# Tile sizes of the prompt loop in a hybrid mLSTM and attention layer: 256 rows at both ends, 512 in the middle

## The reference

```python
h  = rmsnorm(x) * (1 + scale1) + shift1
z  = h @ w_in        # mLSTM q, k, v, o-gate, i-gate, f-gate; attention q, k, v
h_m  = mlstm_chunkwise(...)          # 4 heads x 128, recurrent matrix memory
attn = banded attention, 8 heads x 64, own chunk and 2 chunks before
x  = x + gate1 * (concat(h_m, attn) @ w_out)
x  = x + gate2 * (square(relu((rmsnorm(x) * (1 + scale2) + shift2) @ w_up)) @ w_down)
```

## Time and profile before

| | us |
|---|---|
| median of two runs | 2631.73 |
| the two runs | 2524.87 and 2738.6 |
| the profiled execution | 2528.94 |
| its span on the slowest core (core 5) | 2527.4 |
| spans of the eight cores | 2487.8 to 2527.4 |
| TensorE busy | 1952.1 (77%) |
| VectorE busy | 1124.4 (44%) |
| ScalarE busy | 873.3 (35%) |
| bytes moved by DMA | 267.74 MB, mean 106 GB/s |

### The profile page before, as it was taken

How to read it: one execution, slowest core, us unless ns; L and a number is a source line. 1 busy time by engine, 2 the same in 40 slices (tenths; PEclk the granted TensorE clock), 3 DMA queues, 4 the chain that set the end, 5 groups by cost and what they waited for, 6 DMA issues and landing times.

```text
span 2527.4 us, 33429 instructions; the slowest of 8 cores (2487.8 to 2527.4 us)
## 1 busy us (share of the span) xinstructions
PE 1952.1 (77%) x11094; PEld 917.5 (36%) x11094; DVE 1124.4 (44%) x2546; ACT 873.3 (35%) x2072; POOL 97.4 (4%) x137
## 2 busy tenths in 40 slices
PE   0353577856569798888888888988888889879796
PEld 0121233323324343444433433434444434334343
DVE  2116455544544545444444445454444444454420
ACT  0013465533344324332443334244324333342220
POOL 0000000000000000000000000010000000000101
PEclk9956788878789998999999989999999999999899
DMA  9764995201162235124422522262154225323545
GB/s 239 153 113 68 149 157 109 92 1 51 51 202 84 68 96 171 51 67 139 112 67 84 167 67 67 87 186 62 53 140 126 67 83 154 81 67 93 141 151 122
DMA packets 191866, 267.74 MB, mean 106 GB/s; under 512 B 7148, under 2 KB 168076, under 8 KB 190160
## 3 DMA queue, kind: packets, MB, share of 16 engines
q1 hardware_dynamic: 163840, 201.11, 25.6%
q0 software_dynamic: 27856, 64.50, 15.3%
HBM read 260.96 MB, written 51.38 MB: 124 GB/s over the span
## 4 chain that ended last, share of the span: by engine, by line
PE 56%; DVE 12%; ACT 12%; DMA 11%; issue 8%; DVEq 0%; ACTq 0%; SPq 0%; POOL 0%; POOLq 0%
PE psb L968 13%; PE psb L988 12%; PE psb L701 11%; PE psb L935 5%; PE psb L1007 4%; DVE sb_Eo L855 3%; PE psb L646 3%; DMA ym<-sb_ytmp 3%; DMA sb_uT<-w_in 2%; ACT sb_junk L608 2%; ACT sb_junk L843 1%; DMA sb_x<-xp 1%; ACT sb_qT L612 1%; ACT sb_mixT L923 1%; ACT sb_uT L1120 1%
## 5 line engine op out<-in xcount | busy, mean ns | idle before, releaser
L968 PE MATMUL psb<-sb_h2T,sb_fs 128*128 128x512 bf16 x2048 | 522.0, 396 | 22.3 <-DVE sb_ytmp L994 14.0
L988 PE MATMUL psb<-sb_fs,sb_uT 128*128 128x512 bf16 (+1 forms) x2112 | 505.3, 388 | 15.0 <-DMA sb_fs<-wdn_s 15.0
L701 PE MATMUL psb<-sb_win,sb_hT 128*128 128x512 bf16 (+2 forms) x1576 | 344.1, 366 | 6.4 <-DVE sb_Kp L710 4.2
L988 PEld LDWEIGHTS psb<-sb_fs,sb_uT 128*128 128x128 bf16 (+1 forms) x2112 | 199.5, 99 | 243.6 <-issue 35.9
L968 PEld LDWEIGHTS psb<-sb_h2T,sb_fs 128*128 128x128 bf16 x2048 | 195.4, 101 | 246.2 <-issue 57.9
L972 ACT ACTIVATE sb_uT<-psb 128x512 bf16<-128x512 f32 (+1 forms) x288 | 158.3, 550 | 329.5 <-PE psb L968 326.3
L973 DVE TENSOR_TENSOR sb_uT<-sb_uT 128x512 bf16<-128x512 bf16 (+1 forms) x288 | 112.8, 396 | 280.4 <-ACT sb_uT L972 246.0
L701 PEld LDWEIGHTS psb<-sb_win,sb_hT 128*128 128x128 bf16 (+1 forms) x1576 | 152.2, 99 | 159.5 <-issue 16.0
L935 PE MATMUL psb<-sb_wout,sb_mixT 128*128 128x512 bf16 (+1 forms) x528 | 127.8, 395 | 27.0 <-ACT sb_mixT L923 25.8
L886 ACT ACTIVATE sb_Pm<-psb 128x256 bf16<-128x256 f32 (+1 forms) x264 | 99.7, 378 | 94.7 <-PE psb L881 85.6
L735 DVE SCALAR_TENSOR_TENSOR sb_Chat<-sb_Chat,sb_rho_bc,psb 128x129 f32<-128x129 f32 x260 | 90.2, 347 | 78.9 <-PE psb L730 63.5
(11 more groups left out here) (190 smaller groups left out, 2134.0 us busy)
## 6 DMA issues: line engine op xcount, KB each, us to landing
sb_fs<-wup_s SPq DMA_DIRECT2D x72, 1024.0 KB, 5.3
sb_fs<-wdn_s SPq DMA_DIRECT2D x72, 1024.0 KB, 5.7
sb_x<-xp SPq DMA_DIRECT2D x32, 512.0 KB, 14.8
sb_x<-xm SPq DMA_DIRECT2D x32, 512.0 KB, 5.3
ym<-sb_x POOLq DMA_DIRECT2D x32, 512.0 KB, 5.7
ym<-sb_ytmp POOLq DMA_DIRECT2D x64, 256.0 KB, 4.5
sb_fs<-w_ada POOLq DMA_DIRECT2D x12, 1024.0 KB, 15.5
sb_uT<-w_in SPq DMA_DIRECT2D x8, 1412.0 KB, 11.4
```

Source lines behind the costliest of these rows:

```text
L701: i = e.matmul(pb[0:T, 0:ncols], lhsT=hsrc[:, kc, col_tok0:col_tok0 + T], rhs=win[:, kc, c0:c0 + ncols], start=(kc == 0), stop=(kc == KC - 1))
L968: i = e.matmul(pb[:, 0:NT], lhsT=sl[:, kc, j * 128:(j + 1) * 128], rhs=h2src[:, kc, 0:NT], start=(kc == 0), stop=(kc == KC - 1))
L988: i = e.matmul(pbs[bi][0:T, :], lhsT=uT[:, g * 8 + j, c0:c0 + T], rhs=sl[:, j, :], start=(g == 0 and j == 0), stop=(g == 3 and j == 7))
```

## The change

The list of tile sizes replaces the fixed 512 rows: two tiles of 256 rows (two blocks), six of 512 (four blocks), two of 256, ten tiles in all for the same 4096 rows. norm_T4, thread_B and thread_A take their number of blocks from the tile; gates and qk_feature_major get 256 or 512 columns; ffn_up gets 256 or 512 columns per matmul with the same number of matmuls and the same 16 weight loads per tile; ffn_down has half the matmuls in a small tile, with the same loads. The prefix loop and the sample are as before.

```diff
--- before.py
+++ after.py
@@ -603,16 +603,16 @@
                  r=[dstT.b, modT.b], w=[dstT.b], cost=0.7)
 
         def norm_T4(xts, dstT, n, r):
-            T = 128
-            for b in range(4):
+            nb = len(xts)
+            for b in range(nb):
                 S.op("act", lambda e, b=b: e.activation(out=junk2[:, :], in_=xts[b][:, :], func=AF.Square, accum_out=st4[:, b:b + 1]),
                      r=[xts[b].b], w=[st4.b], cost=1.1)
-            rstd_from_ss(st4[:, 0:4], st4[:, 4:8], D, st4)
-            for b in range(4):
+            rstd_from_ss(st4[:, 0:nb], st4[:, 4:4 + nb], D, st4)
+            for b in range(nb):
                 S.op("act", lambda e, b=b: e.activation(out=xn4[b], in_=xts[b][:, :], func=AF.Identity, scale=st4[:, 4 + b:5 + b]),
                      r=[xts[b].b, st4.b], w=[xn4b[b], (qT.b if b < 2 else kT.b)], cost=1.1)
             base = 0 if n == 0 else 24
-            for pair in range(2):
+            for pair in range(nb // 2):
                 pbs_ = {}
                 for b in (2 * pair, 2 * pair + 1):
                     pbs_[b] = nps()
@@ -1151,19 +1151,32 @@
             S.op("pool", lambda e: e.nop(), r=dram_out_bufs, force=True)
             S.emit()
             return nc
-        n_mt = NM // 512
         curh = [0]
 
+        if NM >= 1536:
+            sizes = [2, 2] + [4] * ((NM - 1024) // 512) + [2, 2]
+        else:
+            sizes = [2] * (NM // 256)
+        tiles = []
+        r0 = 0
+        for nb_ in sizes:
+            tiles.append((r0, nb_))
+            r0 += nb_ * 128
+        assert r0 == NM
+        n_mt = len(tiles)
+
         def thread_B(t):
+            row0, nb = tiles[t]
+            NT = nb * 128
             S.begin()
             xt = xt_next[0]
-            gtail = gates(512, T, 4, defer_tail=True)
-            qk_feature_major(512)
+            gtail = gates(NT, T, nb, defer_tail=True)
+            qk_feature_major(NT)
             gtail()
-            for b in range(4):
-                last = (t == n_mt - 1 and b == 3)
+            for b in range(nb):
+                last = (t == n_mt - 1 and b == nb - 1)
                 cur = curh[0]
-                mixer_block(T, b, b * 128, cur, 128, 0, last, cbf_ready=(b > 0), cbf_next=(b < 3))
+                mixer_block(T, b, b * 128, cur, 128, 0, last, cbf_ready=(b > 0), cbf_next=(b < nb - 1))
                 if last:
                     store("pool", knf, knf[:, :], okp_d)
                     store("pool", vf, vf[:, :], ovp_d)
@@ -1174,26 +1187,27 @@
             S.barrier("up%d" % (t - 1))
             blocks = []
             norm_T4(xt, h2T, 1, 0)
-            for b in range(4):
-                yd = ym_d[t * 512 + b * 128:t * 512 + (b + 1) * 128, :]
+            for b in range(nb):
+                yd = ym_d[row0 + b * 128:row0 + (b + 1) * 128, :]
                 yb = Buf("y"); dram_out_bufs.append(yb)
                 S.op("pool", lambda e, yd=yd, xb=xt[b]: e.dma_start(out=yd, in_=xb[:, :]), r=[xt[b].b], w=[yb], dma="y_" + xt[b].b.name)
                 blocks.append((yd, T, b * 128, yb))
             if t + 1 < n_mt:
-                xt_next[0] = [next_x(xm_d, (t + 1) * 512 + b * 128) for b in range(4)]
+                nrow0, nnb = tiles[t + 1]
+                xt_next[0] = [next_x(xm_d, nrow0 + b * 128) for b in range(nnb)]
                 norm_T4(xt_next[0], hT, 0, 0)
             return S.end(), blocks
 
         def thread_A(t, blocks):
             S.begin()
-            ffn_up(512)
+            ffn_up(tiles[t][1] * 128)
             S.mark("up%d" % t)
             ffn_down(blocks, 0)
             return S.end()
 
         xt_next = [None]
         if n_mt > 0:
-            xt_next[0] = [next_x(xm_d, b * 128) for b in range(4)]
+            xt_next[0] = [next_x(xm_d, b * 128) for b in range(tiles[0][1])]
             norm_T4(xt_next[0], hT, 0, 0)
             Bl, blocks = thread_B(0)
             S.merge(sample_ffn, Bl)
```

## The result

The changed kernel takes 2601.84 us in the median of 12 runs, against 2533.16 us for the kernel before beside it: ratio 1.0274, 95% interval 1.0254 to 1.0294. It is slower by 69 us where 33 were forecast.

The account below looks back on a forecast made before the run. Ends 65% and 98% dense in TensorE work move into pairs 87% dense or worse: ends give back 124 us, pairs take 157. Stages sum to 2560.7, plus 1.5 around the span gives 2562 us, 1.3% slower; range 2492 to 2608.

Parts of the forecast that it names:

- the full pairs: Five stages pairing a 512-row tile's feed-forward with the next 512-row tile's mixer: unchanged at 234.0 us each, 1170 together.
- the pair of FFN(7) with MIX(8): Feed-forward half of tile 7 (four blocks) beside mixer half of tile 8 (two): 172 us, bounds 165 and 178.
- the step that I called my freest: FFN(1), two blocks, beside MIX(2), four blocks: 205 us, lower bound 170, upper 217, output projections 36 us apart.
- The signs that I named beforehand: Opening near 119 us, FFN(1) with MIX(2) 195 to 215, FFN(9) 75 to 90 waiting for loads, middle pairs 234.
- the two small pairs: FFN(0) with MIX(1) and FFN(8) with MIX(9), two blocks each: 120 and 122 us, about half a full pair.
- The slot arithmetic that I made for FFN(9): Last feed-forward: two groups take one 5.5 us load, 3.45 us of matmuls and 0.5 issue, so 4.7 us a group.
- The last FFN: FFN(9), two blocks, alone at the end: 82 us, ends 72 and 99, 34 less than the four-block one.
- The opening: First mixer half, two blocks, beside the sample's feed-forward: 119 us, 80 less than before.
- Packing well: Rival, chance 0.25: FFN(1) with MIX(2) near its TensorE work, 175 us, small pairs 114 each; 2495 us, faster by 34.
- The clock rival: Rival, chance 0.19: TensorE's clock falls in thin stages, adding 17 us in FFN(9), 14 in FFN(1) with MIX(2); 2605 us.
- The rival in which the sample's loads set the opening's end: Rival, chance 0.06: the sample's down projection starts only behind the second mixer block; opening 130 us, sum 2573.
- 87% dense: TensorE work in the five middle full pairs: 203.6 to 205.9 us of 234.0; also priced FFN(1) with MIX(2)'s lower bound, 170.

Follow-up runs that it names:

- thin loads: Changed kernel with each weight load in the 256-row tiles bringing an eighth of its bytes, both projections; ratio 1.002 to the kernel before.
- e8_front_four: Kernel before with only its front split (two 256-row tiles, then seven of 512), four weight slots in the small tiles and for the sample; ratio 0.9973.
- e12_one_each: Kernel before with one 256-row tile at each end, seven of 512 between, four weight slots in small tiles and for the sample; ratio 0.9951.
- e7: Changed kernel with four weight slots in the 256-row tiles, the extra slots' first load no longer waiting for this tile's own results; ratio 1.0087.
- e4: Changed kernel with four weight slots in the 256-row tiles, the extra slots' first load still waiting for this tile's own results; ratio 1.0101.

## Why the prediction was wrong

**Sign and structure held, the size did not.** 33 us forecast, 69 measured. The account, in which the ends give back and the pairs take more, was right in kind. The first norm is 8.0 us shorter on every core, the tail is 14.8, the full pairs, the pair of FFN(7) with MIX(8) (172, measured 171.5) and even the step that I called my freest (205, measured 200.2, with output projections 34 us apart where I had 36) were right. The signs that I named beforehand did not include the small pairs, where the forecast failed.

**The step that failed is the two small pairs**, in which I put the waits for weight loads at nothing. I wrote 112 plus 8 and 117 plus 5, and in the mixer's halves I saw only chains that don't halve. They took 132.6 and 136.6, together 27 us more. The slot arithmetic that I made for FFN(9) (two groups take one load and one group of matmuls) I did not make for their down projections, where eight loads of 1 MB stand beside a quarter of a half-size mixer. The thin loads put 15 and 11 us on it: without most of their bytes the pairs take 117.2 and 125.4, beside the 120 and 122 that were forecast. The sentence that x loads in small tiles find free slots and "can only help" was wrong for the first small pair, where four x blocks are loaded for the next tile and an x store of 9.37 us stands on the chain ahead of a weight load; but it was not costly, as moving the x loads did not shorten the pair.

**The last FFN was mis-sized in the same term.** 82 forecast, 90.2 measured. Loads landed in 7.0 us and not 5.5; here all but the first overlap another load in time, where the last FFN of before had nearly always one at a time and 5.3. Of the groups on the chain, those at a granted clock of 0.55 to 0.70 took 5.1 to 6.5 us and not 3.45 (two of the last FFN's down groups of before had waited for their loads, not one, as I read it). The clock over the stage was 0.84. The opening, 119 forecast and 124.2 measured, had the same loads in its down projection: thin loads for the tile behind it gave 120.1, and four slots for its own 110.1 (e8_front_four) and 112.4 (e12_one_each).

**The comparison with before** adds the rest. The forecast's borders came from one core, whose stages from the opening on sum to 1963.7; the median over eight is 1957.9. Stage by stage the changed kernel is 27 us over the forecast and the kernel before 6 under what I used: 33 + 27 + 6 is 66, of 69 measured; the other 3 are not placed.

**The rivals.** Packing well needed a mixed pair under 185; it was 200, and with no waits for loads to speak of, 198.5, so this rival is out for a reason that it did not know: the pair is held by the mixer's chain, and even 21 us of FFN work less did not shorten it (206.0). The clock rival gave 2605, nearer to the measured 2602 than my 2562, but by luck: its terms were not the ones that came. It put the last FFN at 99 us and half clock throughout (measured 90.2 and 0.84), the mixed pair at 14 more by a clock of 0.80 (it kept 0.90 and took 5 less than my 205), and the small pairs at 6 more each by a clock of 0.85 (their clock was 0.92 and 0.90, and they took 13 and 15 more). It was right that the last FFN's clock would fall. It fell beside the waits for loads: with thin loads it is 0.96, with four slots 0.92 to 0.96 and the stage 65 us. The Trainium skill's rule for thin matmuls that wait for weights (TensorE: Matmul & The Clock Gate, HAM oscillation) stood behind the 99 us case. The trace agrees in direction, with the clock of 0.84; but a 256-row tile with little to wait for (58.2 us at 0.96 with thin loads, about half of the 114.5 of 512 rows) does not need the padding. The rival in which the sample's loads set the opening's end was partly true, with 5 us of its 11: on the chain of the changed kernel's opening stand two waits for these loads, of 7.94 and 9.20 us, and no x store.

**My reading of "87% dense" was wrong**, though it did not hurt the sum. I took it as nearly TensorE-bound and priced moved work by that share. Removing 42 us of TensorE work from a full pair gave 9.7, with the clock down from 0.97 to 0.87; removing 13.4 us of its VectorE chain gave about as much at an unchanged clock.

## What to carry to other kernels

A tile that is halved keeps its weight traffic: before halving, compare one slot's load and one group's matmuls in every stage that the small tile enters, also where other work stands beside it, and count by operations how much that is per load. A busy share near 90% does not say which engine sets the pace; take work off one engine and see, with the granted clock beside it. And give a version that seems to win its control: here the sample's extra slots alone gave all of the front version's gain and about half of the other's.

## What the runs showed of the hardware

Taking matmuls out can make a stage longer: with 192 fewer matmuls in the mixed pair the granted clock went from 0.90 to 0.80, the output projections of the mixer from 3.4 us at 1.00 to between 5.5 and 6.5 us at 0.55 to 0.65, and the pair from 200.2 to 206.0 us (one run; 202.4 to 207.4 on its eight cores, 199.0 to 201.7 with the matmuls in).

With eight cores running the same program, core 6 drew 238 to 249 GB/s in the last FFN with four slots (e7, e4, e12), at a DMA share of 0.89 to 0.95, against 180 with two, at 0.66. So the two-slot version was limited by its waiting and not by the memory. Where loads overlapped, they landed later: 1 MB took a median of 5.3 us when loads came one at a time (the last FFN of before, core 5) and 7.0 when they overlapped (core 6).
